# One fused decoder kernel: attention steps of the first mixer spread over two score banks and three logit places, its convolution one chunk a unit

## What is computed

```python
def _parallel_mixer_layer(x, attn_norm, in_w, ...):
    h = _rmsnorm(x, attn_norm) @ in_w
    q, ckv, iq, ik, iw, z, xbc, dt = _split(h, A_SIZES + B_SIZES)
    y_a = _dsa_attention(q, _rmsnorm(ckv, kv_norm), iq, ik, iw, w_uk, w_uv)
    y_b = _mamba2(z, xbc, dt, conv_w, conv_b, dt_bias, A_log, D, ssm_norm)
    return x + jnp.concatenate([y_a, y_b], axis=-1) @ out_w
```

## Time and profile before

| | |
|---|---|
| Median of 3 runs | 1762.1 us (1760.71 to 1765.19) |
| The profiled execution | 1760.67 us, span 1758.9 us |
| PE busy | 1713.6 us, 97% |
| POOL, DVE, ACT busy | 1067.3, 991.7, 972.1 us |
| Mean granted PE clock | 0.997 of full |

### The profile page before, as it was taken

The page is one execution under the profiler, slowest core; times in us unless marked ns, Lnnn a source line. Parts: engine busy times, 40 slices in busy tenths (PEclk is TensorE's granted clock), DMA queues, the critical chain, the costliest instruction groups (busy, mean ns, idle before and its releaser), DMA issues.

```text
span 1758.9 us, 32213 instructions
## 1 busy us (share of the span) xinstructions
PE 1713.6 (97%) x10886; PEld 1529.7 (87%) x10886; DVE 991.7 (56%) x2116; ACT 972.1 (55%) x1843; POOL 1067.3 (61%) x828
## 2 busy tenths in 40 slices
PE   8989999999999999999999999999999999999999
PEld 8778788888988887999989989899999988888887
DVE  3775433334342335574435999406898766666776
ACT  5556655555465556666436545555555555555554
POOL 8445799997989998975546999997666300000000
PEclk9999999999999999999999999999999999999999
DMA  6223455554545554543524545455444455556774
GB/s 233 96 88 106 159 181 184 191 183 155 188 162 187 190 184 162 195 150 112 203 72 133 183 163 179 165 180 166 165 161 164 159 191 183 187 191 214 232 237 164
DMA packets 91851, 299.00 MB, mean 170 GB/s; under 512 B 10208, under 2 KB 22624, under 8 KB 91520
## 3 DMA queue, kind: packets, MB, share of 16 engines
q1 hardware_dynamic: 91152, 293.64, 49.7%
q0 software_dynamic: 480, 4.35, 0.6%
q10 hardware_dynamic: 144, 0.08, 0.0%
HBM read 290.69 MB, written 7.34 MB: 169 GB/s over the span
## 4 chain that ended last, share of the span: by engine, by line
PE 81%; POOL 9%; issue 4%; DVE 3%; ACT 3%; DMA 0%; POOLq 0%; SPq 0%; DVEq 0%; ACTq 0%
PE bank L684 58%; PE bank L716 9%; POOL w_lo L628 9%; PE bank L717 5%; PE bank L1314 3%; PE bank L662 1%; PE bank L1229 1%; ACT w_hi L1360 1%; PE bank L762 1%; PE bank L776 0%; DMA ring<-stream 0%; DVE arena L2103 0%; PE bank L902 0%; PE bank L1239 0%; ACT h_high_and_low L1376 0%
## 5 line engine op out<-in xcount | busy, mean ns | idle before, releaser
L628 POOL TENSOR_TENSOR w_lo<-ring,w_hi 128x512 fp32r<-128x512 f32 x804 | 1059.8, 1326 | 320.2 <-ACT w_hi L1360 273.7
L1360 ACT ACTIVATE w_hi<-ring 128x512 fp32r<-128x512 f32 x1060 | 666.7, 632 | 690.6 <-PE bank L684 570.3
L684 PE MATMUL bank<-h_high_and_low,w_hi 128*128 128x256 f32 x3552 | 668.6, 286 | 22.2 <-POOL w_lo L628 11.7
L684 PEld LDWEIGHTS bank<-h_high_and_low,w_hi 128*128 128x128 f32 x3552 | 562.8, 192 | 27.8 <-POOL w_lo L628 13.9
L684 PE MATMUL bank<-h_high_and_low,w_lo 128*128 128x256 f32 x1776 | 503.4, 283 | 0.0
L684 PEld LDWEIGHTS bank<-h_high_and_low,w_lo 128*128 128x128 f32 x1776 | 341.7, 192 | 1.0 <-issue 0.7
L684 PE MATMUL bank<-w_hi,A_hi 128*128 128x512 f32 x728 | 287.9, 395 | 1.2 <-DVE A_lo L2600 0.7
L684 PE MATMUL bank<-w_lo,A_hi 128*128 128x512 f32 x728 | 287.7, 395 | 0.0
L684 PE MATMUL bank<-w_hi,A_lo 128*128 128x512 f32 x728 | 287.5, 395 | 0.0
L716 PE MATMUL bank<-h_high_and_low,w_hi 128*128 128x512 f32 x704 | 250.6, 398 | 0.0
L2593 DVE TENSOR_TENSOR w_lo<-ring,w_hi 128x512 fp32r<-128x512 f32 x256 | 177.1, 693 | 120.3 <-ACT w_hi L1360 117.9
(11 more groups left out here) (361 smaller groups left out, 1610.5 us busy)
## 6 DMA issues: line engine op xcount, KB each, us to landing
ring<-stream SPq DMA_DIRECT2D x530, 512.0 KB, 3.3
spill<-mask_parts SPq DMA_DIRECT2D x48, 128.0 KB, 1.7
XN<-spill SPq DMA_DIRECT2D x48, 128.0 KB, 3.3
arena<-branch_w POOLq DMA_DIRECT2D x1, 3072.0 KB, 12.7
X<-x SPq DMA_DIRECT2D x2, 512.0 KB, 4.5
arena<-kv_w SPq DMA_DIRECT2D x1, 1024.0 KB, 5.8
out<-X SPq DMA_DIRECT2D x4, 256.0 KB, 2.1
arena<-row POOLq DMA_DIRECT2D x1, 512.0 KB, 5.0
```

Of the source, the lines that this page charges most:

```text
L628: nc.gpsimd.tensor_tensor(w_lo[:, hs, :], ring[:, slot(phase, e), k * HALF:(k + 1) * HALF], w_hi[:, hs, :].bitcast(F32), ALU.subtract) \
L684: last = mm(dst, a, b, start=start and n == 0, stop=stop and n == 2, skip_group_check=True)
L1360: A(w_hi[:, half_slot(phase, e, k), :], ring[:, slot(phase, e), k * HALF:(k + 1) * HALF], ACT.Copy).then_inc(rounded, 1)
```

## The change

The scores of odd heads go to bank 3, those of even heads stay in bank 0. `LG0` has three places for logits, not two. Transposes come one step later (`attend(i)` takes those of head i-2) and outputs with them (head i-3), on PE, DVE and ACT alike. The 12 chunks use banks 6, 7 and 2 in turn (6 for the last), and `conv` is spread to one chunk a unit with two in unit 9. The choice of keys is spread over five units. `cb` moves from bank 3 and unit 6 to bank 1 and unit 7. `ab0` moves from unit 8, and `inputs_turned` from unit 9 to 10. On ACT `conv_silu` moves from the start of units 6 and 9 to their end, and `decay(0)` behind unit 11. On DVE `segments(0)` and `decay(0)` go behind `conv(11)`. No arithmetic is added or removed.

```diff
-X_BANKS = (6, 7, 2, 3, 6, 7, 6, 7, 6, 7, 6, 7)
+X_BANKS = (6, 7, 2, 6, 7, 2, 6, 7, 2, 6, 7, 6)
...
-        out += [(f"dsa_s{i}", 0, 1), (f"dsa_pT{i}", 4, 1)]
+        out += [(f"dsa_s{i}", (0, 3)[i % 2], 1), (f"dsa_pT{i}", 4, 1)]
...
-    out += [("acs", 1, 1), ("BT", 1, 1), ("cb", 3, 1), ("ab0", 3, 1), ("xsT0", 1, 1), ("xsT2", 2, 1)]
+    out += [("acs", 1, 1), ("BT", 1, 1), ("cb", 1, 1), ("ab0", 3, 1), ("xsT0", 1, 1), ("xsT2", 2, 1)]
...
-        LG0 = a.take(2 * 256, "p (n f) -> p n f", n=2)
+        LG0 = a.take(3 * 256, "p (n f) -> p n f", n=3)
...
-                    if 1 <= i <= NT * H_A:
-                        pe.wait_ge(ev("dsa_weights"), i)
-                        transposes(f"dsa_pT{i - 1}", [LG0[:, (i - 1) % 2, j * P:(j + 1) * P]
-                                                      for j in range((i - 1) // H_A + 1)])
-                    if i >= 2:
-                        t, h = (i - 2) // H_A, (i - 2) % H_A
+                    if 2 <= i <= NT * H_A + 1:
+                        pe.wait_ge(ev("dsa_weights"), i - 1)
+                        transposes(f"dsa_pT{i - 2}", [LG0[:, (i - 2) % 3, j * P:(j + 1) * P]
+                                                      for j in range((i - 2) // H_A + 1)])
+                    if i >= 3:
+                        t, h = (i - 3) // H_A, (i - 3) % H_A
...
                     if u == 6:
                         pe.wait_ge(ev("conv_silu"), 1)
                         transposes("BT", [CV[:, 8 + g, 0:P] for g in range(2)])
+                    if u == 7:
                         pe.wait_ge(*before_turn("cb"))
...
-                    if u == 8:
-                        cumulated(0)
-                    if u == 9:
+                    if u == 10:
                         inputs_turned(0)
                         inputs_turned(2)
 
-                for i in (1, 4):
-                    cumulated(i)
+                cumulated(0)
+                cumulated(1)
+                attend(NT * H_A + 2)
+                cumulated(4)
...
                 for u in range(12):
                     steps = dsa_steps(u)
-                    if u == 6:
-                        conv_silu(0)
-                    if u == 9:
-                        conv_silu(1)
-                    if u == 10:
-                        decay(0)
                     follow("l0_feature", 4 + u, 0, (0,))
                     if len(steps) == 2:
                         attend(steps[0])
                     follow("l0_feature", 4 + u, 0, (1,))
                     attend(steps[-1])
+                    if u == 6:
+                        conv_silu(0)
+                    if u == 9:
+                        conv_silu(1)
...
-                CONVS = {2: (0,), 3: (1,), 4: (2,), 5: (3, 4)}
+                CONVS = ((), (), (0,), (1,), (2,), (3,), (4,), (5,), (6,), (7, 8), (9,), (10,))
                 for u in range(12):
-                    if u >= 6:
-                        conv(u - 1)
                     steps = dsa_steps(u)
-                    attend(steps[0])
-                    for n in CONVS.get(u, ()):
+                    if len(steps) == 2:
+                        attend(steps[0])
+                    if u < 5:
+                        choose(1, (2, 2, 1, 1, 2)[u])
+                    if u == 4:
+                        chosen_mask(1)
+                    for n in CONVS[u]:
                         conv(n)
-                    if u == 6:
+                    attend(steps[-1])
+                    if u == 7:
                         attended(0)
...
-                    if u == 9:
-                        segments(0)
-                    if u == 10:
+                    if u == 11:
                         inputs(0)
                         inputs(2)
-                        decay(0)
 
                 conv(11)
+                segments(0)
+                segments(1)
                 attended(1)
-                segments(1)
                 segments(4)
+                decay(0)
                 decay(1)
```

More of the change, by code:

```diff
@@ L868, in attend @@
                             pe.wait_ge(*before_turn(name))
-                        pe.wait_ge(*read_out(f"dsa_pT{i - 2}"))
+                        pe.wait_ge(*read_out(f"dsa_pT{i - 3}"))
                         for j in range(t + 1):
-                            last = mm(bank(name)[:, h * 64:(h + 1) * 64], PT0[:, i % 2, j * P:(j + 1) * P],
+                            last = mm(bank(name)[:, h * 64:(h + 1) * 64], PT0[:, (i - 3) % 2, j * P:(j + 1) * P],
                                       V0[:, j, h * 64:(h + 1) * 64], start=(j == 0), stop=(j == t))
@@ L1487, in attend @@
                 def attend(i):
[L1489 to L1493, removed]
+                    if 2 <= i <= NT * H_A + 1:
+                        w = P * ((i - 2) // H_A + 1)
+                        act.wait_ge(*full(f"dsa_pT{i - 2}"))
+                        A(PT0[:, (i - 2) % 2, 0:w], bank(f"dsa_pT{i - 2}")[:, 0:w],
+                          ACT.Copy).then_inc(*frees(f"dsa_pT{i - 2}"))
                     if i < NT * H_A:
@@ L1496, in attend @@
                         act.wait_ge(ev("dsa_max"), i + 1)
-                        A(LG0[:, i % 2, 0:w], LG0[:, i % 2, 0:w], ACT.Exp, bias=att[:, i % 4:i % 4 + 1],
+                        A(LG0[:, i % 3, 0:w], LG0[:, i % 3, 0:w], ACT.Exp, bias=att[:, i % 4:i % 4 + 1],
                           accum_out=sums[:, i:i + 1]).then_inc(ev("dsa_weights"), 1)
@@ L2076, in attend @@
                     t, w = i // H_A, P * (i // H_A + 1)
-                    if i >= 2:
-                        dve.wait_ge(*full(f"dsa_pT{i - 2}"))
+                    if i >= 3:
+                        dve.wait_ge(*full(f"dsa_pT{i - 3}"))
                     dve.wait_ge(*full(f"dsa_s{i}"))
-                    V.scalar_tensor_tensor(LG0[:, i % 2, 0:w], bank(f"dsa_s{i}")[:, 0:w], stat[:, 2 + t:3 + t],
+                    V.scalar_tensor_tensor(LG0[:, i % 3, 0:w], bank(f"dsa_s{i}")[:, 0:w], stat[:, 2 + t:3 + t],
                                            MB[:, t, 0:w], ALU.mult, ALU.add).then_inc(*frees(f"dsa_s{i}"))
                     dve.wait_ge(*read_out(f"dsa_s{i}"))
-                    V.tensor_reduce(att[:, i % 4:i % 4 + 1], LG0[:, i % 2, 0:w], AX.X, ALU.max,
+                    V.tensor_reduce(att[:, i % 4:i % 4 + 1], LG0[:, i % 3, 0:w], AX.X, ALU.max,
                                     negate=True).then_inc(ev("dsa_max"), 1)
@@ L2219, in mixer0 @@
                             .then_inc(ev("acs_diff"), 1)
-                    if u == 7:
+                    if u == 8:
                         dve.wait_ge(ev("acs_exp"), 1)
```

7 lines of the change are left out of this document (1 added, 6 removed).

## The result

The changed kernel takes 1772.95 us (median of 4 runs, 1772.27 to 1774.53), the one before 1762.32 on the same chip (4 runs, 1760.71 to 1765.19): 1.006 times as long, 95% interval 1.0042 to 1.0077. That is 10.6 us slower. The profiled execution took 1772.51 us, its span is 1770.8.

The account below looks back on a forecast made before the run. PE, busy 97% of the span, was taken as the bound. From the profiled 1760.67 us, 11.3 of waits and 2.9 of clock go, 18.4 and 6.5 come: 1771.4, nearer the median 1772; range 1764 to 1778.

Parts of the forecast that it names:

- (1): Units 3 and 4: PE waits for `conv(0)` and `conv(1)`, each behind a choice round on DVE; 1.0 and 0.3 us.
- (2): Unit 5: PE waits for `conv(2)`, behind DVE's list from head 6's scores; 3.3 us.
- (3): End of unit 6: `BT` waits for `conv_silu(0)`, on ACT behind head 10's exponential and a table load; 4.4 us.
- (4): Unit 7: `cb` waits for the copy of `BT`; 2.6 us, 1.6 falling earlier on head 8's output, needing `attended(0)`.
- (5): Around unit 10: head 14's transposes wait for the copy of head 13's, 2.7 us, after 0.3 for bank 7.
- (6): First half of `l0_z`: PE waits for bank 3, held by `ab0` until `decay(0)`; 3.8 us.
- new waits: Sum of PE's waits from unit 3 to `l0_z`, none hidden behind another; 18.4 us.
- clock, new: PE at its lower clock after four or five holes of 2.6 to 4.4 us; 6.5 us, bounds 1.4 and 8.6.
- The estimate by it, 1776: Alternative total near 1776 us: the skill's table-switch price adds 1.4 us at each of three waits, 4.2 in all.
- both long waits: Before the change: 2.4 us on score read-out and 5.6 us at unit 6 on `conv(4)`; both claimed to end.
- faster, about 1752: Rival, chance 0.09: spread chunks keep DVE ahead of PE, only two waits on ACT's order stay; sum 1753.5 us.
- The sign of a backlog in unit 4: Unit 4: DVE reading scores there without a backlog would show the prediction wrong; no size given.

Follow-up runs that it names:

- before_filled: Kernel before the change, with 40 extra matmuls whose result nobody reads in the 5.6 us wait ahead of unit 6; 1760.85 us, ratio 0.9985.
- mask_after_conv: Changed kernel with the finished mask on DVE behind `conv(2)` instead of ahead of it in unit 4; ratio 1.0041 to the kernel before.
- silu_ahead: Changed kernel with ACT's `conv_silu(0)` back at the start of unit 6, as before the change; 1768.66 us, ratio 1.0025 to the kernel before.
- reordered: Changed kernel's banks, places and later step, with the lists of PE, DVE and ACT rewritten in the order PE wants results; 1748.65 us, ratio 0.9924.
- reordered_no_later_step: The kernel reordered, with transposes and outputs one step earlier on PE and ACT, DVE's list kept; 1755.9 us, ratio 0.9961 to the kernel before.
- convolutions_unspread: Changed kernel with DVE's order for chunks, choice and mask as before the change; 1774.6 us, ratio 1.0057 to the kernel before.
- decay_ahead: Changed kernel with `decay(0)` on DVE moved ahead of `attended(1)` and `segments(4)`; 1769.94 us, ratio 1.0036 to the kernel before.
- holes_filled: Changed kernel with extra matmuls nobody reads in PE's waits at unit 5, `BT`, head 14's transposes and `l0_z`; 1768.28 us, ratio 1.0027.

## Why the prediction was right

1772.0 was predicted, 1772.95 measured, inside the range. The terms, in its own numbering:

| step | predicted | measured in the profile |
|---|---|---|
| (1) unit 3, unit 4 | 1.0, 0.3 | 0.89, none |
| (2) unit 5 on `conv(2)` | 3.3 | 4.24 |
| (3) `BT` on `conv_silu(0)` | 4.4 | 4.34 |
| (4) `attended(0)` and `cb` | 2.6 | 1.56 + 0.43 |
| (5) bank 7, head 14's transposes | 0.3, 2.7 | none, 2.57 |
| (6) `l0_z` on `decay(0)` | 3.8 | 3.48 |
| new waits | 18.4 | 17.5 |
| clock, new | 6.5 | 6.9 |

- **(1), (4), (5), (6)** were right in mechanism, place and releaser, and 0.3 to 0.6 us too long each; the two small waits named in them, at unit 4 and for bank 7, did not come. (6) was also tested: with `decay(0)` earlier on DVE that wait shrank by the 1.9 us of the two steps, and no other wait moved.
- **(2)** was mis-sized: the term "DVE 0.55 + 0.59 + 1.96 + 0.78 + 2.47" took the mask at 0.78 from a trace in which POOL was idle beside it. With POOL at work it is 0.94 longer, which is the whole error (4.24 - 3.3). That the sum of the waits came within 0.9 us is in part luck: this term was 0.9 too short, the others together 1.8 too long.
- **(3)** was right to 0.1, and is the longest single wait: undoing it shortens the stretch by 4.9. The ACT timeline shows the order that the step named, the exponential of head 10, then the table load, then the silu, started 0.02 us after the load ends. (The list of ACT after the change, shown with the change, likewise begins at head 10's exponential and not at head 9's, and the one of before ends at the table load for head 9's.)

```profile
99.39 0.51 ACT L1498 ACTIVATE arena<-arena,att 128x256 f32<-128x256 f32 x1 [1.07 <-DVE att L2083]
99.80 0.19 ACT L1498 ACTIVATION_READ_ACCUMULATOR arena<-arena,att 128x1 f32 x1
100.00 1.28 ACT L1511 ACT_TABLE_LOAD   x1
101.30 1.06 ACT L1511 ACTIVATE arena<-arena 128x1024 f32<-128x1024 f32 x1
```

  So a change of tables costs the load alone here (1.28 us). The Trainium skill (ScalarE: Activation LUTs, "What ACT_TABLE_LOAD costs") counts a drain of about 1380 ns beside each load. The estimate by it, 1776, did not come true: no such gap stands ahead of the load at 100.00 or between it and the silu.
- **What was removed**: both long waits went, as said. That others took their place is the heart of the case. The rival "faster, about 1752" (its own sum gives 1753.5) needed DVE to reach each `conv` as soon as its unit is used. The prediction named DVE's list between head 6's scores and unit 5 as the evidence against it, and there it failed (4.24 at unit 5). The sign of a backlog in unit 4 holds for head 7, whose scores PE began at 80.98 and DVE read at 86.00; head 6's were read at once, as the 0.55 in (2) has it.
- **The clock** was right in size (6.9 read, 5.7 given back by filling four of the holes) and nearly so by hole: three of the four cost 1.4 to 1.6 us, near the 1.4 taken for each, and unit 5's cost 2.5. Which unit pays varies between executions, as before_filled and mask_after_conv show, so agreement to some tenths is not to be counted on.

The ratios do not follow the stretches closely. By ratio, mask_after_conv is 3.3 us faster than the changed kernel and its stretch 0.8 shorter, silu_ahead 6.2 against 4.9. Two things stand behind it. The kernel before, by which each is divided, has medians from 1762.3 to 1764.9 us; by their own medians the two are 1.2 and 4.3 us faster than 1772.95. And the clock also falls in a later stage, in some executions and not in others. The profiled execution of silu_ahead (1771.85 us, the slowest of its 12) has 0.83 from 798 to 818 us, the changed kernel's 1.00, with waits of 1.5 and 1.2 us in that stage in both:

```profile
798.00:818.00 20.00, 19.63 (x141) 0.83 0.28 99
```

```profile
798.00:818.00 20.00, 19.43 (x168) 1.00 0.29 107
```

From the end of the stretch to the end of the span that execution took 1600.5 us. Nine of the twelve profiles took 1596.3 to 1596.7 there, the kernel before and the changed one among them, so nothing behind the stretch moved with the edits. The other two of the twelve, before_filled and reordered, took 1597.9, with 0.99 from 778 to 978 us. What makes the clock fall there in one execution and not in the next stays open.

## What to carry to other kernels

More banks, buffers or slack in a pipeline take away only the wait that was seen; in this case what PE waited for next was set by the order of work on the engines that feed it. Lay that order out from PE's next need backwards, instruction by instruction with prices from the trace, and look above all at a long piece (a chunk, a table load with its activation) put in front of a short one that somebody needs. The same banks and the same later step cost 0.6% in one order and gave 0.8% in another. Whether that other order would have gained as much with the banks of before was not run.

## What the runs showed of the hardware

**A DVE instruction with two tensor inputs in SBUF (TENSOR_TENSOR) is held up while POOL rounds weights.** The mask's second instruction (128x256) took 0.43 us in the five of twelve profiles in which POOL was idle beside it (before, before_filled, reordered_no_later_step, convolutions_unspread, and mask_after_conv, where it was moved there on purpose). In the other seven it fell into a rounding on POOL and took 1.37 to 1.40; in the changed kernel it ended 0.28 us after POOL's instruction. A small one (128x16, L2217) took 0.56 beside POOL in the changed kernel, ending 0.03 us after POOL's, and 0.17 in the kernel before with POOL idle. A chunk's step at L2103, which reads PSUM for one input, took 0.48 at 75.97, with POOL at work, as did all 24 instructions of that line in the changed kernel. The Trainium skill (SBUF — State Buffer, "Who interferes with whom") says that an instruction with two SBUF inputs contends with one of GpSimd that reads SBUF, and the page describes the shared ports as an exclusive lock; the trace agrees, by these numbers.

**The clock's price is not one number per hole.** In the changed kernel a hole of 4.24 us cost 2.5 us behind it, one of 4.34 cost 1.4, one of 2.57 cost 1.4 and one of 3.48 cost 1.6; in decay_ahead one of 1.6 us in front of `l0_z` cost nothing that shows (3.00 us for the half, and 2.99 behind one of 0.52 in holes_filled). A hole of 0.89 us at unit 3 cost nothing in the changed kernel (3.07 us for the unit), and in mask_after_conv, with the same work ahead of it, 1.65 us (4.63 against 2.98).
